# Key-value state copies by sample and bias heads by two, given out over eight projection rounds

## The chip, the cores and the metric

The kernel runs on one core of one Trainium2 chip. The metric is device time in microseconds, median of the runs. TensorE does the matrix products, VectorE and ScalarE move and convert tiles, GpSimd issues stores, SyncE issues loads. Loads and stores that SyncE issues go through the DMA queue called q1 in the profile, those that ScalarE issues through q10, those of GpSimd through q0. All three queues are served by the same 16 DMA engines.

## The reference

One inference step of a two-layer decoder trunk, for a prompt group of 512 rows and a sample group of 8 rows (520 columns in all). Layer 0 is attention with sparse branches; before it stands one large input projection. Layer 1 is a gated short convolution. What matters here:

```python
def att_project(h, w_in):
    proj = h @ w_in                 # 520 x 2048 by 2048 x P_ATT
...
def att_sample(h, ..., s_win_k, s_win_v, ...):
    k_w = jnp.concatenate([s_win_k, kw], axis=1)
    v_w = jnp.concatenate([s_win_v, vw], axis=1)
...
    return out, (kc, vc, ks, vs, k_w[:, tn:], v_w[:, tn:], kb, vb, ki)
...
def dense_attention(q, t, k, v, s, tbl, window):
    n = t[:, None] - s[None, :]
    bias = jnp.transpose(tbl[rel_bucket(n)], (0, 2, 3, 1))[None]
```

So two outputs, the window states of keys and of values, are the old states shifted by one row: for each of 8 samples, 511 rows of 256 numbers are copied unchanged from input to output, 4088 KB for each state. And the softmax logits get a bias that depends on the distance of query and key, one table for each of 16 heads.

## The kernel before

The program is a sequence of stages with a barrier of all engines between them. The change lies in `stage_project`, the second stage, which runs from about 130 to 1030 us of the span. It computes the input projection as 66 tiles of 128 output columns. For each tile, 2048 x 128 weights (1 MB) are loaded into one of four buffers `k.w`. ScalarE makes a high part of them (`Split.hi`, L128, writes `w_high`), VectorE the low part (`Split.lo`, L133, writes `w_low`), and TensorE multiplies in three passes (L146: 16 row blocks, 3 products, 2 halves of the columns). ScalarE copies one half of the result out of PSUM (L609), VectorE the other (L646), and GpSimd stores the tile to `k.proj` (L672).

Between the projection tiles the stage computes the modulation vectors of adaLN: one slot for each of tiles 0 to 63, with 1 MB of `w_ada` loaded into the same ring of four buffers and 16 small matmuls (L178). So a projection tile takes two entries of the ring, and the ring holds the entries of two tiles. Four tiles and four slots are one round. After the fourth tile of a round ScalarE also copies the round's modulation rows out (L185, `keep_rows`), and a round later TensorE turns them (L192).

All loads stand in one order on SyncE (L155): for each tile its projection weights, then its modulation weights. Each is issued when the buffer has come free, the projection weights' buffer by `w_low` and the modulation weights' buffer by the slot's last matmul.

The rounds run in segments, `SEGS`: a segment of one round is written out, one of more rounds is a loop on each engine. Before, these are rounds 0, 1 to 3, 4, 5 to 13, and 14 and 15. Between segments an engine may do something more.

In program order ScalarE does for tile t: `hi` of tile t + 1 (it waits for the load and for tile t - 1's matmuls), then the copy out of tile t. Whatever stands in ScalarE's order ahead of a `hi` delays the high part, then the low part, then TensorE.

Two blocks of DMAs stand in ScalarE's order, and nothing inside the stage reads what they write:

- `spread`, behind round 3 (tile 15). It stores the table of 16 bias heads (640 numbers each) to DRAM, waits for it to land, then issues 16 DMAs, one for each head, that write the head 128 times with a row step of 641 into `bias_skew` (320 KB each, DRAM to DRAM, L626). Stage `stage_attend_prompt` reads them a millisecond and more later.
- `move`, behind round 4 (tile 19). It issues two DMAs, DRAM to DRAM, each of 8 samples x 511 rows x 256 numbers (L618).

At the end of the stage ScalarE waits until all of them have landed.

Of the kernel before, what the change touches and what calls it, by code (L numbers as in the profile page):

```python
# [19 lines left out]
P = 128  # L20
D = 2048
# [3 lines left out]
NS = 8  # L25
# [4 lines left out]
NH = 8  # L30
# [4 lines left out]
WIN = 512  # L35
# [32 lines left out]
BREV = 640  # L68
# [300 lines left out]
def project_entry(t):  # L369

    return 32 + 8 * (t // 4) + 2 * (t % 4) if t < 64 else 160 + t - 64
# [147 lines left out]
def stage_project(k):  # L519
# [4 lines left out]
    gate_w_in, moved, hot_in, heads_mm, heads_kept, heads_out = (k.sem("pj_" + n) for n in ("gate_w_in", "moved", "hot_in", "heads_mm", "heads_kept", "heads_out"))  # L524
    sp_ = Split(k, project_entry, 2)

    SEGS = [(0, 1, 0, 0, 2 * D), (1, 4, 512, 0, 2 * D + 512), (4, 5, 2048, 1, 0), (5, 14, 2584, 1, 512), (14, 16, 7208, 1, 10 * 512)]

    def rounds(eng, body, *more):
        for seg in SEGS:  # L530
            if seg[1] - seg[0] == 1:
                body(0, seg)
            else:
                with eng.Fori(0, seg[1] - seg[0]) as j:
                    body(j, seg)
            for at, what in more:
                if at == seg[1]:
                    what()

    with ExitStack() as ctx:  # L540
# [5 lines left out]
        with nc.Block() as block:  # L546

            @block.sync
            def _(sp):
                w = k.i["w_in_att"]  # L550

                def body(j, seg):
                    first, _, col, layer, acol = seg
                    for s in range(4):
                        if first == 0 and s < 2:
                            continue
                        n = project_entry(4 * first + s)
                        load_weights(k, sp, n, w[0, :, bass.ds(j * 512 + (col + s * P), P)], j, 2)
                        load_weights(k, sp, n + 1, k.i["w_ada"][layer, s * 512:(s + 1) * 512, bass.ds(j * 512 + acol, 512)], j, 2)

                rounds(sp, body)
                load_weights(k, sp, project_entry(64), w[0, :, RUNS[2][1] + 8 * P:RUNS[2][1] + 9 * P])
                n = project_entry(65)
                sp.wait_ge(k.w_free[n % 4], n // 4)
                wg = k.w[:, n % 4, :].rearrange("p (a n) -> p a n", n=P)
                sp.dma_start(wg[:, :, 0:WI_ROW], k.i["w_in_att"][0, :, GA_COL:GA_COL + WI_ROW].rearrange("(a p) n -> p a n", p=P)).then_inc(k.w_in[n % 4], 16)
                sp.dma_start(wg[:, :, WI_ROW:P], k.i["w_in_att"][0, :, WI_COL:WI_COL + NI].rearrange("(a p) n -> p a n", p=P)).then_inc(gate_w_in, 16)
# [32 lines left out]
            @block.scalar  # L600
            def _(act):

                def step(t, j, first=False, last=False):
                    if not last:
                        sp_.hi(act, t + 1, j)
                    act.wait_ge(sp_.used, j * 4 + (t + 3))
                    if not first:
                        act.wait_ge(stored[t % 4], j * 16 + 16 * (t // 4))
                    nc.scalar.activation(out[:, t % 4, 0:HC], ps[:, t % 2 * 2, 0:HC], ACT.Copy).then_inc(kept_a, 1)  # L609

                def body(j, seg):
                    for s in range(4):
                        step(4 * seg[0] + s, j, first=(seg[0] == 0))
                    ada.keep_rows(act, project_entry(4 * seg[0] + 3) + 1, seg[0], j, 2)

                def move():
                    for name in ("win_k", "win_v"):
                        act.dma_start(k.o[name + "_s"][0, :, 0:WIN - 1], k.i["state_nsa_" + name][0, :, 1:WIN]).then_inc(moved, 16)  # L618

                def spread():  # L620

                    act.wait_ge(heads_kept, 2)
                    act.dma_start(k.bias_heads.rearrange("(h c) -> h c", c=BREV), heads[:, :]).then_inc(heads_out, 16)
                    act.wait_ge(heads_out, 16)
                    for h in range(2 * NH):
                        act.dma_start(bass.AP(k.bias_skew.tensor, h * P * (BREV + 1), [[BREV + 1, P], [1, BREV]]), bass.AP(k.bias_heads.tensor, h * BREV, [[0, P], [1, BREV]])).then_inc(moved, 16)  # L626

                act.dma_start(k.table[:, :], k.i["rel_bias"]).then_inc(hot_in, 16)
                act.dma_start(hot[:, :], k.i["hot"][:, 0:T]).then_inc(hot_in, 16)
                sp_.hi(act, 0)  # L630
                rounds(act, body, (4, spread), (5, move))
                act.wait_ge(gate_w_in, 16)
                step(64, 0)
                step(65, 0, last=True)
                act.wait_ge(moved, 32 + 16 * 2 * NH)

            @block.vector
            def _(dve):
# [1591 lines left out]
def build(nc, ins, outs):  # L2230
    with ExitStack() as ctx:
# [25 lines left out]
        with ExitStack() as layer0:  # L2257
# [4 lines left out]
            with ExitStack() as projecting:  # L2262
                k.split_buffers("0", projecting)
                with k.stage():
                    stage_front(k)
                with k.stage():
                    stage_project(k)
# [108 lines left out]
```

## Time and profile before

| | |
|---|---|
| median of 3 runs | 3528.1 us (3526.4 to 3530.64) |
| profiled execution, its own time | 3524.6 us |
| its span | 3523.0 us |
| granted TensorE clock, mean | 0.914 |
| TensorE matmul busy | 3045.3 us (86%) |
| DMA, mean over the span | 144 GB/s |

The profile gives, for one execution, each engine's instructions with start and duration, what ended the idle time before them, and the DMA packets by queue. The granted clock is that of TensorE: 1.00 is its upper level of 2.4 GHz and 0.50 its lower one of 1.2 GHz. A matmul's end is modelled, so a busy TensorE need not be one at its peak. DMA shares are of all 16 engines over the stretch. Packets are what one DMA engine moves in one piece.

### The profile page before, as it was taken

How to read it: one execution, taken by the hardware profiler on the slowest of the kernel's cores; microseconds unless marked ns; L12 is line 12 of the kernel's file. 1: busy time of each engine (PE TensorE's matmuls, PEld its weight loads, DVE VectorE, ACT ScalarE, POOL GpSimd, SP SyncE). 2: the span in 40 equal slices, each digit the busy share in tenths (PEclk: the TensorE clock that was granted, in tenths of full speed). 3: DMA queues.
4: the chain of work that ended last, by engine and by line, in shares of the span. 5: the costliest groups of instructions: out<-in, count | busy, mean ns of one | idle time of the engine just before them, and what ended most of it. 6: DMA issues, size and time to landing. Idle time of an engine off the chain costs nothing. (4 is left out here: it accounts for less than half of the span.)

```text
span 3523.0 us, 57162 instructions
## 1 busy us (share of the span) xinstructions
PE 3045.3 (86%) x22272; PEld 2671.5 (76%) x22272; DVE 1355.6 (38%) x2192; ACT 724.8 (21%) x1089; POOL 107.5 (3%) x149
## 2 busy tenths in 40 slices
PE   6799789999975889797886776699799999998796
PEld 3599779999963488685443554599799999998796
DVE  2321122212214278464342666622543344343333
ACT  2211111111102021220000433311422222221212
POOL 0000000000000000000000112100000000000000
PEclk8799889999987899998877886799999999999898
DMA  9766766666634641424977224431333333330621
GB/s 339 225 177 199 236 199 181 176 183 188 188 109 133 196 119 48 123 76 148 299 231 227 73 73 138 130 99 45 89 101 90 101 95 96 101 93 27 176 64 49
DMA packets 592962, 496.73 MB, mean 141 GB/s; under 512 B 36908, under 2 KB 515645, under 8 KB 591597
## 3 DMA queue, kind: packets, MB, share of 16 engines
q1 hardware_dynamic: 526872, 408.45, 39.8%
q10 hardware_dynamic: 58128, 60.58, 5.3%
q0 software_dynamic: 7840, 26.10, 1.8%
q8 instruction: 73, 1.20, 0.1%
q14 instruction: 49, 0.40, 0.0%
HBM read 460.02 MB, written 48.70 MB: 144 GB/s over the span
## 5 line engine op out<-in xcount | busy, mean ns | idle before, releaser
L146 PE MATMUL psum<-h_high,w_high 128*128 128x260 f32 x5184 | 1057.9, 285 | 106.6 <-DVE w_low L133 56.2
L146 PE MATMUL psum<-h_high,w_low 128*128 128x260 f32 x5184 | 1049.2, 284 | 0.0
L146 PE MATMUL psum<-h_low,w_high 128*128 128x260 f32 x5184 | 1047.8, 284 | 0.0
L146 PEld LDWEIGHTS psum<-h_high,w_high 128*128 128x128 f32 x5184 | 804.5, 190 | 150.4 <-issue 93.7
L146 PEld LDWEIGHTS psum<-h_high,w_low 128*128 128x128 f32 x5184 | 804.2, 190 | 0.0
L146 PEld LDWEIGHTS psum<-h_low,w_high 128*128 128x128 f32 x5184 | 803.3, 190 | 0.0
L133 DVE TENSOR_TENSOR w_low<-w,w_high 128x2048 fp32r<-128x2048 f32 x162 | 371.0, 2291 | 580.0 <-ACT w_high L128 579.7
L128 ACT ACTIVATE w_high<-w 128x2048 fp32r<-128x2048 f32 x162 | 309.3, 1910 | 500.5 <-PE psum L146 391.6
L646 DVE COPY pj_out<-psum 128x260 f32<-128x260 f32 x66 | 28.3, 429 | 525.8 <-PE psum L146 525.8
L609 ACT ACTIVATE pj_out<-psum 128x260 f32<-128x260 f32 x66 | 25.6, 387 | 673.0 <-PE psum L146 673.0
L178 PE MATMUL psum<-w,c 128*32 128x512 f32 x768 | 110.7, 659 | 29.6 <-DMA w<-in_w_ada 21.0
L1395 DVE COPY at_kt<-psum 128x512 f32<-128x512 f32 x144 | 93.4, 686 | 63.1 <-PE psum L1466 62.6
L1078 PE MATMUL psum<-w,cz_xtk 128*128 128x256 f32 x512 | 117.2, 390 | 0.0
L1078 PE MATMUL psum<-w_v,cz_xtv 128*128 128x256 f32 x512 | 117.2, 390 | 0.0
L1078 PEld LDWEIGHTS psum<-w,cz_xtk 128*128 128x128 f32 x512 | 115.3, 308 | 0.4
L1078 PEld LDWEIGHTS psum<-w_v,cz_xtv 128*128 128x128 f32 x512 | 115.3, 308 | 0.4
L1994 DVE TENSOR_TENSOR ou_t<-psum,adaT 128x8 f32<-128x8 f32 x32 | 5.3, 166 | 232.5 <-PE psum L146 232.5
L2160 DVE RECIPROCAL cv_parts<-cv_parts 128x520 f32<-128x520 f32 x16 | 54.4, 3402 | 78.9 <-ACT cv_parts L2114 78.9
L1731 PE MATMUL psum<-pa_ptA,pa_vA 128*128 128x128 f32 x320 | 54.6, 308 | 16.5 <-ACT pa_ptA L1773 16.5
L1731 PEld LDWEIGHTS psum<-pa_ptA,pa_vA 128*128 128x128 f32 x320 | 46.7, 215 | 26.4 <-ACT pa_ptA L1773 21.5
L672 POOL DMA_DIRECT2D proj<-pj_out x66 | 35.9, 544 | 987.9 <-DVE pj_out L646 987.9
L868 PE MATMUL psum<-ip_k,ip_q 128*128 128x128 f32 (+3 forms) x128 | 38.5, 455 | 30.1 <-DMA ip_q<-proj 30.1
(361 smaller groups left out, 2667.1 us busy)
## 6 DMA issues: line engine op xcount, KB each, us to landing
w<-in_w_ada SPq DMA_DIRECT2D x96, 1024.0 KB, 6.3
w<-in_w_in_att SPq DMA_DIRECT2D x65, 1024.0 KB, 9.2
w<-in_w_in_conv SPq DMA_DIRECT2D x64, 1024.0 KB, 6.3
proj<-pj_out POOLq DMA_DIRECT2D x66, 260.0 KB, 5.4
cz_pgk<-in_cache_nsa_cmp_k SPq DMA_DIRECT2D x128, 128.0 KB, 2.2
cz_pgv<-in_cache_nsa_cmp_v SPq DMA_DIRECT2D x128, 128.0 KB, 2.2
w<-in_w_out_att SPq DMA_DIRECT2D x16, 1024.0 KB, 6.0
w<-in_w_out_conv SPq DMA_DIRECT2D x16, 1024.0 KB, 6.1
```

The costliest lines, as they stand in the source:

```text
L128: act.activation(k.wh[:, s % 2, :], k.w[:, n % 4, :], ACT.Copy).then_inc(self.high, 1)
L133: dve.tensor_tensor(k.wl[:, s % 2, :], k.w[:, n % 4, :], k.wh[:, s % 2, :].bitcast(F32), ALU.subtract).then_inc(k.w_free[n % 4], 1)
L146: mm = pe.matmul(k.psum[:, banks + hf, 0:HC], w[:, kt, :], x[:, kt, hf * HC:(hf + 1) * HC], start=(kt == 0 and m == 0), stop=(kt == KT - 1 ...
L178: mm = pe.matmul(k.psum[32 * a:32 * a + 32, self.bank, :], k.c32[:, q * 4 + a, :], k.w[:, n % 4, a * 512:(a + 1) * 512], start=(q == 0), s ...
L609: nc.scalar.activation(out[:, t % 4, 0:HC], ps[:, t % 2 * 2, 0:HC], ACT.Copy).then_inc(kept_a, 1)
L646: dve.tensor_copy(out[:, t % 4, HC:TC], ps[:, t % 2 * 2 + 1, 0:HC]).then_inc(kept_v, 1)
L672: pool.dma_start(tile, out[:, t % 4, :]).then_inc(stored[t % 4], 16)
L868: mm = pe.matmul(ps[:, 4 * b + i, 0:P * (i + 1)], q[:, b, i * P:(i + 1) * P], ki[:, 0:P * (i + 1)], start=True, stop=True)
L1078: mm = pe.matmul(ps[:, b, 0:CH], rows, w1[:, l, :], start=(l == 0), stop=(l == CB - 1))
L1395: eng.tensor_copy(kt[:, s % 2, :, c * 256:(c + 1) * 256], ps[:, 3 + q % 2, :].rearrange("p (g q) -> p g q", g=G)).then_inc(kept, 1)
L1731: mm = pe.matmul(ps[:, o, i * P:(i + 1) * P], hv[:, r % SL, br, c, :], pt[:, v % ring, c * P:(c + 1) * P], start=(not A and v % UH == 0 an ...
L2160: dve.reciprocal(e[:, :], e[:, :]).then_inc(zrecip, 1)
```

## The change

The DMAs of both blocks are given out over rounds 5 to 12. At the end of each of these rounds, behind `keep_rows`, ScalarE issues four DMAs: the key state and the value state of one sample (sample j in the j-th of these rounds), and two bias heads (2j and 2j + 1). The store of the head table stays behind round 3, without the wait for its landing; this wait now stands in each round ahead of the bias heads' DMAs. To get a segment of eight rounds, round 13 becomes a segment of its own. The bytes that are moved, and all that is computed, are the same. The bias heads' access patterns are written in another form with the same rows of 640 numbers.

```diff
-    SEGS = [(0, 1, 0, 0, 2 * D), (1, 4, 512, 0, 2 * D + 512), (4, 5, 2048, 1, 0), (5, 14, 2584, 1, 512), (14, 16, 7208, 1, 10 * 512)]
+    SEGS = [(0, 1, 0, 0, 2 * D), (1, 4, 512, 0, 2 * D + 512), (4, 5, 2048, 1, 0), (5, 13, 2584, 1, 512), (13, 14, 2584 + 8 * 512, 1, 9 * 512), (14, 16, 7208, 1, 10 * 512)]
...
                     ada.keep_rows(act, project_entry(4 * seg[0] + 3) + 1, seg[0], j, 2)
-
-                def move():
-                    for name in ("win_k", "win_v"):
-                        act.dma_start(k.o[name + "_s"][0, :, 0:WIN - 1], k.i["state_nsa_" + name][0, :, 1:WIN]).then_inc(moved, 16)
-
-                def spread():
-
+                    if seg[0] == 5:
+                        copies(j)
+
+                def pass_heads():
                     act.wait_ge(heads_kept, 2)
                     act.dma_start(k.bias_heads.rearrange("(h c) -> h c", c=BREV), heads[:, :]).then_inc(heads_out, 16)
+
+                def copies(j):
+
+
+                    for name in ("win_k", "win_v"):
+                        act.dma_start(k.o[name + "_s"][0, bass.ds(j, 1), 0:WIN - 1], k.i["state_nsa_" + name][0, bass.ds(j, 1), 1:WIN]).then_inc(moved, 16)
                     act.wait_ge(heads_out, 16)
-                    for h in range(2 * NH):
-                        act.dma_start(bass.AP(k.bias_skew.tensor, h * P * (BREV + 1), [[BREV + 1, P], [1, BREV]]), bass.AP(k.bias_heads.tensor, h * BREV, [[0, P], [1, BREV]])).then_inc(moved, 16)
+                    skew = k.bias_skew.rearrange("(h p c) -> h p c", p=P, c=BREV + 1)
+                    rows = k.bias_heads.rearrange("(h c) -> h c", c=BREV).unsqueeze(1)
+                    for i in range(2):
+                        act.dma_start(skew[bass.ds(j * 2 + i, 1), :, 0:BREV], rows[bass.ds(j * 2 + i, 1)].broadcast_to([1, P, BREV])).then_inc(moved, 16)
...
-                rounds(act, body, (4, spread), (5, move))
+                rounds(act, body, (4, pass_heads))
...
-                act.wait_ge(moved, 32 + 16 * 2 * NH)
+                act.wait_ge(moved, 16 * 4 * NS)
```

## Rows read from the trace of the kernel before

**Rows 1.** Stretches of the stage: us, busy us of each engine, granted clock, DMA share, GB/s
```profile
338.40:390.14 51.74, 44.04 (x350) 40.24 (x350) 9.99 (x9) 9.46 (x9) 2.17 (x4) 0.93 0.84 243
...
425.00:449.00 24.00, 3.41 (x16) 1.94 (x16) 0.00 (x0) 0.00 (x0) 0.00 (x0) 0.56 0.57 225
...
454.00:460.00 6.00, 6.00 (x34) 6.00 (x35) 2.59 (x3) 1.91 (x1) 0.54 (x1) 0.64 1.06 344
...
480.45:532.19 51.74, 51.74 (x428) 47.84 (x431) 10.99 (x9) 9.41 (x9) 2.17 (x4) 1.00 0.63 183
```

**Rows 2.** ScalarE in order of time, an undisturbed round: start us, us, instruction
```profile
480.45 0.39 ACT L609 ACTIVATE pj_out<-psum 128x260 f32<-128x260 f32 x1 [10.52 <-PE psum L146]
...
532.19 0.39 ACT L609 ACTIVATE pj_out<-psum 128x260 f32<-128x260 f32 x1 [10.52 <-PE psum L146]
533.30 0.60 ACT L185 ACTIVATE ada_rows<-psum 128x512 f32<-128x512 f32 x1 [0.72 <-PE psum L178]
533.79 1.92 ACT L128 ACTIVATE w_high<-w 128x2048 fp32r<-128x2048 f32 x1
```

**Rows 3.** ScalarE in order of time, the last undisturbed round's end
```profile
997.85 0.39 ACT L609 ACTIVATE pj_out<-psum 128x260 f32<-128x260 f32 x1 [10.52 <-PE psum L146]
```

**Rows 4.** ScalarE in order of time, round 4, behind the bias heads' DMAs
```profile
338.40 0.39 ACT L609 ACTIVATE pj_out<-psum 128x260 f32<-128x260 f32 x1 [10.52 <-PE psum L146]
...
344.13 11.14 ACTq L626 DMA_DIRECT2D bias_skew<-bias_heads  x16
355.38 1.91 ACT L128 ACTIVATE w_high<-w 128x2048 fp32r<-128x2048 f32 x1 [15.28 <-issue]
...
399.24 0.39 ACT L609 ACTIVATE pj_out<-psum 128x260 f32<-128x260 f32 x1 [10.52 <-PE psum L146]
```

**Rows 5.** ScalarE in order of time, round 5, behind the states' DMAs
```profile
400.27 0.79 ACTq L618 DMA_DIRECT2D out_win_k_s<-in_state_nsa_win_k  x1
401.10 0.71 ACTq L618 DMA_DIRECT2D out_win_v_s<-in_state_nsa_win_v  x1
402.08 1.92 ACT L128 ACTIVATE w_high<-w 128x2048 fp32r<-128x2048 f32 x1 [1.21 <-issue]
412.03 0.39 ACT L609 ACTIVATE pj_out<-psum 128x260 f32<-128x260 f32 x1 [8.04 <-PE psum L146]
449.64 1.91 ACT L128 ACTIVATE w_high<-w 128x2048 fp32r<-128x2048 f32 x1 [37.23 <-DMA w<-in_w_in_att]
```

**Rows 6.** Waits of TensorE, first in 340 to 380 us, then in 400 to 480: total, times, longest
```profile
PE psum L146 <- DVE w_low L133: 7.7, 1, 7.7
...
PE psum L146 <- DVE w_low L133: 23.3, 1, 23.3
PE psum L178 <- DMA w<-in_w_ada: 2.6, 1, 2.6
```

**Rows 7.** SyncE's issues in order of time: start us, us that the issue took
```profile
339.42 0.37 SPq L155 DMA_DIRECT2D w<-in_w_ada  x1
339.83 0.51 SPq L155 DMA_DIRECT2D w<-in_w_in_att  x1
...
413.10 31.35 SPq L155 DMA_DIRECT2D w<-in_w_ada  x1
```

**Rows 8.** DMA queues, 400 to 450 us: packet sizes, then queue, packets, MB, share
```profile
DMA packets 3431, 11.91 MB, mean 238 GB/s; under 512 B 88, under 2 KB 2257, under 8 KB 3302
...
q10 hardware_dynamic: 144, 8.37, 38.7%
```

**Rows 9.** DMA queues, 340 to 400 us
```profile
q10 hardware_dynamic: 2336, 5.28, 30.3%
```

**Rows 10.** DMA in 505.87 to 557.61 us, an undisturbed round: tenths in 40 slices, landing
```profile
DMA  0469999800008899993000599999100269999900
...
w<-in_w_in_att SPq DMA_DIRECT2D x4, 1024.0 KB, 9.1
```

**Rows 11.** The bias heads' DMAs by tile name: issue ns min/median/max
```profile
L626 ACTq DMA_DIRECT2D bias_skew<-bias_heads x16: 612/619/1388, 344.1 to 353.9; - x16
```

## The prediction

> **What bounds the kernel now.** I read the busy time by stretches over the projection stage first, then ScalarE's instructions in order of time, then TensorE's waits, then the DMA queues. In an undisturbed round TensorE is busy for 51.74 of 51.74 us at the full granted clock, and the 16 DMA engines are busy for 0.63 of it [rows 1]. So the stage is bound by TensorE's matmuls. The copies out of PSUM by ScalarE are a clock for it: they mark the end of each tile. The ends of round 5 and round 6 are 532.19 - 480.45 = 51.74 us apart [rows 2], and the nine rounds up to 997.85 us take (997.85 - 532.19) / 9 = 51.74 us each [rows 3]. Nothing is to be won or lost there except by keeping TensorE waiting.
>
> Two rounds are not like that. Round 4 ends 399.24 - 338.40 = 60.84 us after round 3 [rows 4], which is **9.1 us** over the normal 51.74. Round 5 ends 480.45 - 399.24 = 81.21 us after round 4 [rows 2, 4], **29.5 us** over. Together 38.6 us of an otherwise even stage. They have different causes, and it matters which part of the change removes which.
>
> *Round 4 is late because of ScalarE's order, not of bandwidth.* A `hi` normally starts 533.79 - 532.19 = 1.60 us after the last copy of a round [rows 2], so here it should start at 340.00. It starts at 355.38, behind the wait for the head table and 11.14 us of issuing 16 DMAs [rows 4]: 15.4 us late. TensorE then waits 7.7 us for `w_low` [rows 6]. So a `hi` at this place may come 15.4 - 7.7 = **7.7 us** late before TensorE notices. The other 1.4 us of the 9.1 is the granted clock, 0.93 in this round [rows 1].
>
> *Round 5 is late because of the transfers.* Issuing the two state copies took 0.79 + 0.71 us, the `hi` behind them came at 402.08, and the next copy out came 412.03 - 399.24 = 12.79 us after the last [rows 4, 5], a normal tile. The damage comes after it: SyncE's next load issue is held for 31.35 us [rows 7], a `hi` waits 37.2 us for its weights [rows 5], TensorE waits 23.3 + 2.6 us [rows 6], and its granted clock is 0.56 from 425 to 449 us and still 0.64 from 454 to 460 [rows 1]. That the clock falls to its lower level of 1.2 GHz while TensorE idles is part of the 29.5 us, since I read the loss from tile ends.
>
> What the copies do to the DMA engines: q10 moves 8.37 MB in 144 packets and takes 38.7% of 16 engines in 50 us, which is 0.387 x 50 x 16 = **310 engine-us** [rows 8]. 3431 - 3302 = 129 packets of all queues are 8 KB and longer, so the data went in about 128 packets of 65 KB, 2.4 us each. The stall of 37 us fits these 310 engine-us spread over 8 engines (38.7 us), one for each sample, and not over 16 (19.4 us). For most of this time the loads behind them hardly move. The bias heads took 0.303 x 60 x 16 = **291 engine-us** on q10 [rows 9], in packets of 5.28 MB / 2336 = 2.3 KB.
>
> **The change, part by part.**
>
> *Removed behind round 3.* The wait for the head table and the 16 issues go; one issue of the head table stays. The `hi` there returns to its place and 9.1 us are gained, with the clock's dip.
>
> *Removed behind round 4.* Both state copies go, with the 29.5 us and the clock that they cost.
>
> *Added: ScalarE's issue time in rounds 5 to 12.* Behind `keep_rows`, ahead of the next `hi`: two state issues of at most 0.79 and 0.71 us [rows 5] and two bias heads at 0.619 us median [rows 11], 2.7 us together. The upper bound takes the longest seen for all four, 4 x 1.39 = 5.6 us [rows 11]; the issues now compute their addresses from the loop counter, which no ScalarE row here shows (SyncE's, which do the same, take 0.37 us [rows 7]). Both ends are under the 7.7 us of slack. What is queued behind them is one `hi`, then VectorE's `lo`, then TensorE's next tile but one; the running tile is their cover. Cost nothing; the price beyond 7.7 us would be 8 times the excess. The wait for the head table in each round is for a store issued over 100 us before: nothing.
>
> *Added: DMA work in rounds 5 to 12.* Each round gets an eighth of both: 310 / 8 = 38.7 and 291 / 8 = 36.4 engine-us, 75 in all. A round has 51.74 x 16 = 828 engine-us and uses 0.63 of them, 522; with the copies 597, or 0.72. There is room on the average. But it could be late in one burst, so the slack of one load counts. The load of projection weights issued at 339.83 [rows 7] lands 9.1 us later by the median [rows 10], at 348.9. It is used by the `hi` behind the copy out of the next tile, which is due 12.79 us after the copy at 338.40, at 351.2, and 0.3 us later begins: 2.6 us of slack, and then the 7.7 us that a `hi` has. A load may be **10.3 us** late. If all of a round's copies stood ahead of it on evenly used engines, it would be 75 / 16 = 4.7 us late. If the state copies fell on 8 engines, as they do now, it would be 38.7 / 8 + 36.4 / 16 = 7.1 us. Both are covered; the digits of the round show two to four empty slices of 1.3 us behind each tile's loads [rows 10], and there the engines catch up before the next tile. I take nothing, with an upper end of 2.5 us a round, 20 us, for a share that lies badly. Less than nothing isn't possible, as undisturbed rounds have TensorE busy throughout.
>
> *How many engines one sample's copy takes* is the one number that the trace doesn't show, since here each copy has 8 samples. The Trainium skill, "DMA: Bandwidth & Descriptors", section "Why a DMA increments its semaphore by 16 and not by 1", says that a DMA is spread over the largest k up to 16 that divides the slowest dimension larger than 1, and that a contiguous run in a single dimension can be cut so that it spreads. By that rule the copy before has k = 8, for its 8 samples, and the trace agrees (310 engine-us in a stall of about 37 us). For one sample it would give 16 if the run is cut, and if it is not, 1; the sum above would stand with 16 and fall with 1, and no row here shows which.
>
> *The segments.* Round 13 written out in place of a pass of the loop costs nothing: the stretch from 532.19 to 997.85 us crosses such a border, behind round 13, at an even 51.74 us a round [rows 2, 3].
>
> *The end of the stage.* The last copies are issued behind round 12, three rounds (155 us) ahead of the wait for them. Nothing.
>
> *The sum* against the profiled execution: 3524.6 - 9.1 - 29.5 = 3486.0 us. The runs' median is 3.5 us above that execution, so the forecast for the median is 3528.1 - 38.6 = 3489.5; with half a microsecond for small delays, **3490.0**.
>
> **The rivals.**
>
> *A. The copies leak.* Both stalls go, but in each of the eight rounds TensorE waits a little: a load comes more than 10.3 us late, or a `hi` more than 7.7. For: loads and copies will be issued side by side, since SyncE's loads come 1.4 us behind a round's last copy out (339.83 against 338.40) and ScalarE's DMAs 1.0 us behind it (400.27 against 399.24) [rows 4, 5, 7]; the round's DMA share rises to 0.72, and a held SyncE issue delays all later ones in its order [rows 7]. Against: the sums above leave 3 us even at 8 engines. At 0.5 to 2.5 us a round it gives 3494 to 3510.
>
> *B. One sample's copy runs on one engine.* The place: the engine that gets all of it. It has 0.63 x 51.74 = 32.6 us of weights and stores in a round, plus 38.7 us of states, plus 2.3 us of bias heads: 73.6 us, against 51.74. Each weight load is spread over all engines and complete only when the slowest has done its part, so each round would last 73.6 us at least: 8 x 21.9 = 175 us more, 3490 + 175 = 3665 us. If weights stand still while such a copy runs, as they do now, each round costs what `move` costs now, 29.5 us, and the time is 3490 + 236 = 3726. The point from which it decides is the load's slack: 38.7 / n + 2.3 exceeds 10.3 us for n of 4 engines and fewer; at 4 it is 1.7 us a round, a case of A, at 2 it is 11.4 us a round, 91 us. Against: 8 packets of 65 KB for each sample could as well go to 8 engines, and an even cut is natural for a contiguous run. The skill's rule named above gives this result if the run isn't cut. Time 3665 to 3726, slower.
>
> *C. Issuing costs more inside the loop.* If the four issues take more than 7.7 us, the stall of round 4 comes back eight times. At 9 us, 1.3 x 8 = 10 us plus clock dips of 1.4 x 8 = 11: 3511. Against: 1.39 us is the longest of 16.
>
> *D. It doesn't do what it says.* The stalls would have to come from something that stays. Both begin right behind the moved instructions, and the undisturbed rounds before and after have none; if only the 9.1 us went, the time would be 3519.
>
> **How the numbers follow.** Forecast, 3484 to 3494: 0.70. A: 0.14. B, with two engines as well, which ends slower too: 0.08. C: 0.05. D: 0.03. Predicted time 3490.0. The range 3484 to 3511 holds the forecast, most of A and part of C, about 0.85. A measurement of this kernel can tell 0.2%, 7 us, from no change; B alone ends slower, and of A, C and D only a few hundredths lie near zero: faster 0.90, within 0.2% 0.02, slower 0.08.
>
> **What would show it.** Right: all rounds 51.7 us apart; no wait of TensorE for `w_low` over 1 us in the stage; granted clock 1.00 from 184 us to the stage's end; DMA share near 0.72 in rounds 6 to 13; about 3 us of issuing behind each `keep_rows` and a `hi` about 5 us behind the round's last copy out; no SyncE issue over a few us. Wrong: rounds 6 to 13 evenly longer, with a `hi` waiting for `w` (A or B; the length and number of q10's packets tell them apart) or with the `hi` late by issue (C). It would also be wrong if a later stage changed its length, for which I have no reason.

## The result

The changed kernel takes **3484.0 us** (median of 4 runs, 3478.7 to 3486.9) against 3527.7 us before (3526.4 to 3530.6 in the 4 runs of this comparison): ratio 0.9873, 95% interval 0.9856 to 0.9890. That is 43.8 us less. The forecast was 3490.0 (a gain of 38.6 us, less half a microsecond for small delays), with a range that began at 3484. The median lies 6.0 us under the forecast and a hair outside the range (unrounded 3483.99), and the gain is 5 us larger than the sum says. The profiled execution took 3484.61 us, 40.0 under that of before.

Stretches of the projection stage, after (us, busy us of PE, PEld, DVE, ACT, POOL, granted clock, DMA share, GB/s); rounds 4, 5, 6 and 7. They answer to [rows 1]:

```profile
338.90:390.64 51.74, 51.74 (x428) 47.84 (x431) 11.08 (x10) 9.47 (x10) 2.17 (x4) 1.00 0.64 185
390.64:442.38 51.74, 51.74 (x428) 47.85 (x431) 10.99 (x10) 9.35 (x10) 2.16 (x4) 1.00 0.64 184
442.38:494.12 51.74, 51.74 (x428) 47.85 (x431) 10.99 (x10) 9.59 (x10) 2.16 (x4) 1.00 0.71 216
494.12:545.86 51.74, 51.74 (x428) 47.84 (x431) 10.99 (x10) 9.58 (x10) 2.16 (x4) 1.00 0.72 216
```

Rounds 4 and 5, 60.84 and 81.21 us before, are 51.74 us like their neighbours, the clock stays at its upper level, and the DMA share in the rounds with copies is 0.71 to 0.72. TensorE waits for nothing between 150 and 960 us. ScalarE in order of time, after, at the end of round 6; it answers to [rows 2, 4, 5]:

```profile
494.12 0.39 ACT L609 ACTIVATE pj_out<-psum 128x260 f32<-128x260 f32 x1 [10.52 <-PE psum L146]
495.22 0.60 ACT L185 ACTIVATE ada_rows<-psum 128x512 f32<-128x512 f32 x1 [0.72 <-PE psum L178]
495.45 0.54 ACTq L626 DMA_DIRECT2D out_win_k_s<-in_state_nsa_win_k  x1
496.24 0.54 ACTq L626 DMA_DIRECT2D out_win_v_s<-in_state_nsa_win_v  x1
497.02 1.36 ACTq L631 DMA_DIRECT2D bias_skew<-bias_heads  x2
498.91 1.92 ACT L128 ACTIVATE w_high<-w 128x2048 fp32r<-128x2048 f32 x1 [3.09 <-issue]
506.91 0.39 ACT L609 ACTIVATE pj_out<-psum 128x260 f32<-128x260 f32 x1 [6.08 <-PE psum L146]
511.91 1.92 ACT L128 ACTIVATE w_high<-w 128x2048 fp32r<-128x2048 f32 x1 [4.61 <-DMA w<-in_w_in_att]
519.53 0.39 ACT L609 ACTIVATE pj_out<-psum 128x260 f32<-128x260 f32 x1 [5.70 <-PE psum L146]
```

The four issues and what lies between them take 2.9 us (495.45 to 498.38), and the `hi` behind them starts 4.8 us behind the round's last copy out where 1.6 is normal. The next `hi` waits 4.6 us for its weights, which are late because of the copies. Both delays are used up before TensorE: the copies out are 12.79 and 12.62 us apart. DMA queues in this round, after (kind: packets, MB, share of 16 engines):

```profile
q10 hardware_dynamic: 352, 1.70, 8.8%
```

0.088 x 51.74 x 16 = 73 engine-us, where the forecast had 75. The 1.05 MB of the two states went in 32 packets of 32.7 KB, which is each state cut into 16. They took 38.8 engine-us between 500.31 and 503.39 us, so at least 13 engines ran at once: the copy of one sample runs on 16 engines, not on 8 and not on one.

So the projection stage did what the forecast said, within 0.2 us. From barrier to barrier it takes 869.5 us instead of 908.3, 38.8 less. What is left open is the other part of the gain, and it lies outside the stage. The stage of mixer A's prompt attention, whose program text is the same, took 204.9 us before and 201.9 after.

### The profile page after: what moved, and what is told of

It is laid out like the page before. It is cut to its first block and busy times, and to the rows that moved or that the text cites. A ratio compares the mean times of both kernels' runs of the same rounds, so it can differ in the third digit from the quotient of the medians.

```text
span 3483.0 us, 57217 instructions
## 1 busy us (share of the span) xinstructions
PE 3043.6 (87%) x22272; PEld 2668.6 (77%) x22272; DVE 1355.1 (39%) x2192; ACT 726.5 (21%) x1089; POOL 107.2 (3%) x149
## 5 line engine op out<-in xcount | busy, mean ns | idle before, releaser
L873 PE MATMUL psum<-ip_k,ip_q 128*128 128x128 f32 (+3 forms) x128 | 39.0, 459 | 29.9 <-DMA ip_q<-proj 29.9
```

The costliest lines, as they stand in the source:

```text
L873: mm = pe.matmul(ps[:, 4 * b + i, 0:P * (i + 1)], q[:, b, i * P:(i + 1) * P], ki[:, 0:P * (i + 1)], start=True, stop=True)
```

## The experiments

Each run was timed beside the kernel before on the same chip; "before" below is its median there. The length of a stage is read from barrier to barrier in the profiled execution.

### Is the surplus real, and do the two halves add up?

The changed kernel once more:

> The changed kernel once more, timed in five rounds beside the kernel before. The forecast's sum (theory S: the two stalls of 9.1 and 29.5 us and nothing else) gives before minus 38.6 us. The first comparison gave 3527.7 - 3484.0 = 43.8 us, 5 us more. If this surplus is only the spread of a few executions (theory N), the difference here lies between 37 and 41 us. If something in later stages is really faster (theory L), it is again 42 to 46 us, and the prompt attention stages are again 3.0 and 1.7 us shorter in the trace than before.

Measured: 3482.0 us against 3524.4, 42.4 less, ratio 0.9883 (0.9868 to 0.9899). Projection stage 869.5 us; mixer A's prompt attention 201.3. The surplus is there again, as theory L said. The interval of this one comparison, 35.6 to 46.5 us, holds 38.6 too, so by itself it doesn't rule out chance; the comparisons below do.

The halves alone. Only the states given out:

```diff
                     act.dma_start(k.bias_heads.rearrange("(h c) -> h c", c=BREV), heads[:, :]).then_inc(heads_out, 16)
+                    act.wait_ge(heads_out, 16)
+                    for h in range(2 * NH):
+                        act.dma_start(bass.AP(k.bias_skew.tensor, h * P * (BREV + 1), [[BREV + 1, P], [1, BREV]]), bass.AP(k.bias_heads.tensor, h * BREV, [[0, P], [1, BREV]])).then_inc(moved, 16)
 
                 def copies(j):
...
-                    act.wait_ge(heads_out, 16)
...
-                    for i in range(2):
-                        act.dma_start(skew[bass.ds(j * 2 + i, 1), :, 0:BREV], rows[bass.ds(j * 2 + i, 1)].broadcast_to([1, P, BREV])).then_inc(moved, 16)
```

> Only the state copies are given out over the rounds; the 16 bias heads stay in one block behind round 3. By the forecast only the stall of round 5 goes: 29.5 us less than before, and round 4 keeps its 9.1 us (ScalarE's hi 15 us late, TensorE waiting 7.7 us for w_low). If the two stalls had one common cause in the DMA queues, round 4's stall would shrink or the gain would not be 29.5 us.

Measured: 3492.9 us, 31.6 less than before's 3524.4, ratio 0.9901 (0.9886 to 0.9916). Stage 880.9 us, 27.4 less than 908.3; round 5 is 51.74 us long, round 4 is 62.93 (340.42 to 403.35), a stall of 11.2 us and not of 9.1.

And only the bias heads given out (`move` as before, behind round 4):

> Only the bias heads are given out, two a round; the state copies stay in one block of two DMAs behind round 4. By the forecast 9.1 us less than before, round 4 at 51.74 us and round 5 still about 81 us long. The sum of this gain and that of the other half is 38.6 us if the parts are independent.

Measured: 3509.9 us, 14.5 less, ratio 0.9962 (0.9949 to 0.9976). Stage 900.6 us, 7.7 less; round 4 is normal, round 5 takes 81.5 us, a stall of 29.8. The two stalls are separate, as the forecast had them. But the halves gain 31.6 and 14.5 us by their times and 27.4 and 7.7 by their stages, and both stage gains lie under the intervals of the times (29.6 to 40.2 and 8.5 to 18.0 us). The surplus stands in both halves, which speaks against either group of DMAs as its cause.

Does it hang on when the later stages start?

```diff
...
                 act.wait_ge(moved, 16 * 4 * NS)
+                act.wait_ge(sp_.used, NTILES + 2)
+                for i_ in range(20):
+                    act.wait_ge(idled, (i_ + 1))
+                    act.activation(idle[:, :].rearrange("p (a n) -> p a n", n=T), k.xT[:, 0:4, 0:T], ACT.Copy).then_inc(idled, 1)
```

> The changed kernel with 20 activations of 1.9 to 2.0 us each, one after another, on ScalarE at the end of the projection stage, all other engines idle: 38 to 40 us are put back, so that the later stages start about when they do in the kernel before. Theory S or N: the time is that of the changed kernel plus the 38 to 40 us, so 0 to 2 us from before. Theory L with a cause in what the change left behind for later stages: about 5 us under before still. Theory L with a cause in when the later stages start (the granted clock in the attention stages, where it moves between its two levels): the surplus goes and the time is before's.

Measured: the 20 activations take 38.8 us, but 7.6 us of that lie beside the last tile's store; the stage takes 900.7 us, 31.2 more than in the changed kernel. Time 3514.4 us, 10.1 under before, where its stage is 7.6 under 908.3. Against the changed kernel it is 32.3 us longer for 31.2 us of stage. The later stages now start within 8 us of where they do before and their surplus is 2.5 us by this count, which is too little to tell by time. The trace tells more: mixer A's prompt attention takes 200.2 us, as in the changed kernel, so the start time isn't what makes it shorter.

### Where the surplus comes from

All variants so far share one thing beside the DMAs, the new segments. Two kernels test it: the kernel before again, and the kernel before with this line alone:

```diff
-    SEGS = [..., (5, 14, 2584, 1, 512), (14, 16, 7208, 1, 10 * 512)]
+    SEGS = [..., (5, 13, 2584, 1, 512), (13, 14, 2584 + 8 * 512, 1, 9 * 512), (14, 16, 7208, 1, 10 * 512)]
```

> The kernel before, profiled a second time. The stage of mixer A's prompt attention took 204.9 us in the first trace of before and 199.6 to 201.9 in the five traces of the changed kernel and its variants so far. Theory N (the granted clock of that stage differs from run to run, whatever the kernel): it lies between 199 and 205 us here, as like to be low as high. Theory P (something in the program of before makes it longer): about 205 us again.

> The kernel before with the new segments alone: round 13 written out, no DMA moved. All variants so far have these segments, and all their later stages together were about 4 us shorter than before's by the medians. The forecast prices the segments at nothing: the projection stage as long as before, 908 us, and the time within 2 us of before's. Theory P with the program's layout as its cause (code lies at other addresses in all later stages): 3 to 5 us less than before, outside the projection stage.

Measured: before again 3524.8 us, ratio 0.9997 (0.9988 to 1.0007), that attention stage 203.4 us. Segments alone **3517.3 us, 7.8 less, ratio 0.9974 (0.9965 to 0.9982)**, the stage 197.7 us. No DMA is moved, and still it is faster. (The projection stage of this execution is not shorter but 3.4 us longer than 908.3, in the two stalls.) The step "The segments" of the forecast is the one that fails.

The trace shows the place. VectorE in that stage, the kernel before (start us, us, instruction, idle time before it and what ended it):

```profile
2030.07 0.29 DVE L1790 CUSTOM_DVE_ANT_0 pa_sA<-psum,pa_tA 128x128 f32<-128x128 f32 x1 [3.08 <-issue]
...
2034.18 0.11 DVE L1827 MEMSET pa_lcA<- 128x64 f32 x1 [3.62 <-issue]
```

and TensorE behind it:

```profile
2037.17 1.02 PE L1711 MATMUL psum<-const,pa_lcA 128*16 128x128 f32 x4 [5.53 <-DVE pa_lcA L1851]
```

The same three places with the segments alone:

```profile
2030.71 0.29 DVE L1790 CUSTOM_DVE_ANT_0 pa_sA<-psum,pa_tA 128x128 f32<-128x128 f32 x1 [2.55 <-issue]
...
2031.31 0.11 DVE L1827 MEMSET pa_lcA<- 128x64 f32 x1
```

```profile
2034.31 1.02 PE L1711 MATMUL psum<-const,pa_lcA 128*16 128x128 f32 x4 [2.54 <-DVE pa_lcA L1851]
```

"issue" means that the engine waited for nothing that the profile shows. Before, VectorE stands 3.08 us and then again 3.62; with the segments, once, 2.55. TensorE's wait for the result shrinks by 3.0 us. It isn't a hidden wait for TensorE: the one product that the program makes the memset wait for (`cqk`, L1699) was ready at 2026.49 us, over 7 us before the memset. The waits of VectorE for "issue" in this stage (total us, times, longest) are, in the kernel before:

```profile
DVE pa_lcA L1827 <- issue: 4.1, 2, 3.6
DVE pa_sA L1790 <- issue: 3.1, 1, 3.1
```

and in the changed kernel:

```profile
DVE pa_sA L1795 <- issue: 2.5, 1, 2.5
```

7.2 us against 2.5: **4.7 us**. It is the same in three traces of before, and like the changed kernel (2.5 to 2.8 us, no wait ahead of the memset) in all 13 traces of kernels with the new segments in VectorE's program. The whole stage agrees: with VectorE's old program it takes 203.1 to 206.0 us in five traces, with the new one 197.4 to 202.1 in 13, and the means are 4.6 us apart.

What moves it? Every engine has its own program, so round 13 can be written out for one engine and left in the loop for another (`for seg in (SPLIT if eng is nc.vector else ONE_LOOP)` and its opposite). Three kernels, the third being the changed kernel with VectorE's loop left as it was:

> The kernel before, with round 13 written out in VectorE's program alone; the other engines keep the loop of nine rounds, no DMA is moved. In both traces of before VectorE stands 4.1 to 4.2 us (twice) ahead of its memset of pa_lcA in the prompt attention stage, waiting for nothing that the profile shows, and in none of eight traces of kernels with the new segments. Theory V (where VectorE's instructions lie in its own program decides this): the standstill is gone, that stage takes 198 to 202 us and not 203 to 205, and the kernel is 4 to 8 us faster than before. Theory W (it hangs on another engine's program or on the whole program's length): the standstill stays and the time is before's.

> The kernel before, with round 13 written out in every engine's program but VectorE's. Theory V: the standstill of 4.1 us stays and the time is within 2 us of before's. Theory W: it goes, and the kernel is 4 to 8 us faster. If TensorE's 197 added instructions had a share of their own, the time would lie between.

> The changed kernel, but VectorE keeps its loop of nine rounds as before; all DMAs are given out as in the changed kernel. Theory V: the standstill of 4.1 us is back, and the gain over before is the forecast's 38.6 us (37 to 40.5), not 42 to 44. Theory W: as the changed kernel, 3482 us or 42 to 44 us under before.

Measured, with before at 3527.9 us:

| round 13 written out | time | ratio, 95% interval | that stage |
|---|---|---|---|
| for VectorE alone | 3520.2 us | 0.9980 (0.9971 to 0.9989) | 199.4 us |
| for all but VectorE | 3526.1 us | 0.9994 (0.9985 to 1.0003) | 204.8 us |
| changed kernel, all but VectorE | 3485.1 us | 0.9882 (0.9867 to 0.9897) | 203.1 us |

The waits for "issue", in this order:

```profile
DVE pa_sA L1791 <- issue: 2.5, 1, 2.5
```

```profile
DVE pa_lcA L1828 <- issue: 4.6, 2, 4.1
DVE pa_sA L1791 <- issue: 3.1, 1, 3.1
```

```profile
DVE pa_lcA L1833 <- issue: 4.1, 2, 3.6
DVE pa_sA L1796 <- issue: 3.1, 1, 3.1
```

The standstill follows VectorE's program and nothing else, each time as theory V said. The written-out round has 15 rows of VectorE's in the trace (9 of them work on tiles) and 424 matmuls with as many weight loads of TensorE's: the few take the standstill away, the many don't. (The 197 of the expectation stands in no trace.) The third kernel's time is a miss: 42.8 us under before, where 37 to 40.5 were expected. Timed beside it, the changed kernel with the same packets (`states_on_4_engines` below) took 3481.3 us, 3.8 less than its 3485.1, which is the right sign and near 4.7 us; but both are medians of four runs, and the interval of its gain, 36.3 to 46.9 us, holds 38.6 as well as 43.3. So that the standstill costs time is shown on the kernel before, where VectorE's program alone is worth 7.7 us; how much of the changed kernel's surplus it makes up is not.

Why it stands: in the traces an 8 KB packet of the DMA queue named "instruction" runs inside each such standstill. Queues in the kernel before from 2026.9 to 2030.1 us, and from 2030.5 to 2034.1:

```profile
q14 instruction: 2, 0.02, 2.1%
```

```profile
q14 instruction: 1, 0.01, 1.1%
```

With the segments alone there is one in the remaining gap (2028.1 to 2030.7 us) and the second gap is not there. That VectorE waited for its own next instructions, and that a few more of them moved a border of such a block away from this place, fits all of it. But a packet of this queue doesn't always go with a standstill: with the segments alone one runs at 2033.06 us, while VectorE works on without a gap, and the profile doesn't say for which engine a packet is. That the standstill follows VectorE's layout is shown; that the packet is the cause is only argued from its timing.

A third trace of before, to see how much its two stalls spread:

> The kernel before, profiled a third time. Rounds 4 and 5 together lost 38.6 us in both traces of before, and 38.2, 41.7 and 41.8 us in three kernels that issue the same blocks of DMAs. If that is spread from one execution to the next, this trace may show either 38 or 42 us, and the mean of them, about 40, is what the forecast should have put down; if the program decides it, it is 38.6 again. VectorE's standstill ahead of its memset of pa_lcA is 4.1 us again by theory V.

Measured: 3527.8 us, ratio 1.0006 (0.9996 to 1.0016). Rounds 4 and 5 lost 38.5 us (their `keep_rows` start 141.95 us apart, against 2 x 51.74), and the standstill is 4.1 us. So the three traces of before agree on 38.5 to 38.6. In two of the three kernels that issue the same blocks and differ only in the segments it was 41.7 and 41.8 us (38.2 in the third), the excess being in round 4. Over all seven traces that keep the block of bias heads, round 4 takes 60.3 to 60.8 us where the engines other than VectorE keep the loop of nine rounds (before three times, and `split_vector_only`), and 62.9 to 63.5 where they don't (`segments_only`, `split_all_but_vector`, `states_in_rounds`). The block itself is slower there: the `hi` behind it starts 17.8 to 18.7 us after the last copy out and not 15.9 to 17.0, TensorE waits 8.5 to 9.4 us for `w_low` and not 6.6 to 7.7, and the granted clock of the round is 0.92 and not 0.94. So this too seems to go with a program's layout, perhaps ScalarE's; no run tests it, and it can't touch the changed kernel, which has no such block.

### Are the prices of the stalls right?

The forecast had a slack of 7.7 us for a `hi` behind a round, 10.3 us for a load, and a rule: the loads stand still for as long as the copies ahead of them take on their engines. First the `hi`, made later by activations behind each round's DMAs (two and four of them):

> The changed kernel with two more activations (1.94 us each, one after another) on ScalarE behind each round's four DMAs, so the next hi comes 3.2 + 3.9 = 7.1 us later than in an undisturbed round. By the forecast's slack of 7.7 us TensorE doesn't notice: rounds of 51.7 us, the time of the changed kernel. If the slack is smaller by more than a microsecond, each of eight rounds is longer by the excess.

> The same with four activations: the hi comes 3.2 + 7.8 = 11.0 us late, 3.3 over the slack of 7.7. By the forecast's rule eight rounds lose 3.3 us each, 26 us, and up to 1.4 us more each for the granted clock, 26 to 38 us in all. If ScalarE's order had no such edge (VectorE or TensorE could run on), less.

Measured: with two 3482.7 us (0.9882, 0.9863 to 0.9900), stage 869.5 us, the `hi` 6.5 us late and no wait of TensorE. With four 3504.0 us (0.9931, 0.9916 to 0.9946), about 22 over the changed kernel. Its rows:

```profile
499.10 0.39 ACT L610 ACTIVATE pj_out<-psum 128x260 f32<-128x260 f32 x1 [10.52 <-PE psum L146]
...
503.46 7.76 ACT L620 ACTIVATE pj_idle<-xT 128x2048 f32<-128x2048 f32 x4 [2.65 <-issue]
511.12 1.89 ACT L128 ACTIVATE w_high<-w 128x2048 fp32r<-128x2048 f32 x1
```

The `hi` comes 12.02 - 1.60 = 10.4 us late, so 10.4 - 7.7 = 2.7 us should show. TensorE's waits in the stage:

```profile
PE psum L146 <- DVE w_low L133: 22.6, 8, 3.5
```

Seven of the eight waits are 2.7 to 2.8 us, and there the clock stays at 1.00 and the round is 2.8 us longer. In the first round the `hi` was 11.2 us late; TensorE waited 3.5 us, the granted clock of that round was 0.97, and the round was 4.9 us longer. So the slack of 7.7 us is right to a tenth at both latenesses, and the further 1.4 us for the clock came with the wait of 3.5 us and not with those of 2.8. The stage is 24.7 us longer than in the changed kernel, a little under the 26 to 38 expected.

Then the load. The first try wrote each sample's state as 4 rows:

> The changed kernel, with each sample's state written as 4 rows of two pieces of 65 KB, so that the copy runs on 4 DMA engines. The forecast's rule for a load's slack: the loads behind the copies are late by 38.7 / 4 + 2.3 = 12.0 us where 10.3 are covered, so TensorE waits 1.7 us in each of eight rounds, 14 us, and up to 1.4 us more each for the granted clock: 3496 to 3507 us. If loads stood still for less than the copies' whole time, the time is that of the changed kernel, 3482; if a held issue of SyncE costs more than the copy's own time, it is more than 3510.

Measured: 3481.3 us, ratio 0.9867 (0.9852 to 0.9882), but it tests nothing: the trace has 32 packets of 32.7 KB a round on 16 engines, as in the changed kernel. Here a contiguous run was cut in the same way when it was written down as 4 rows. It counts as one more run of the changed kernel. So the next two copy rows that aren't contiguous, 63 rows of 4 (or 2) samples at a time:

```diff
                     for name in ("win_k", "win_v"):
-                        act.dma_start(k.o[name + "_s"][0, bass.ds(j, 1), 0:WIN - 1], k.i["state_nsa_" + name][0, bass.ds(j, 1), 1:WIN]).then_inc(moved, 16)
+                        for b in range(0, NS, 4):
+                            act.dma_start(k.o[name + "_s"][0, b:b + 4, bass.ds(j * 63, 63)], k.i["state_nsa_" + name][0, b:b + 4, bass.ds(j * 63 + 1, 63)]).then_inc(moved, 16)
```

> The changed kernel, but each round copies 63 rows of 4 samples at a time (two DMAs for each state; 7 rows remain and go out behind round 13). The slowest dimension is 4, so each DMA runs on 4 engines, the same ones, with packets of 64.5 KB. By the forecast's rule the loads are late by 38.7 / 4 + 2.3 = 12.0 us, 1.7 over the slack, 14 to 25 us over eight rounds: 3496 to 3507 us. The issues cost 4 x 0.55 + 1.4 = 3.6 us, covered. If the rule is too strict (the loads behind go on while the copies run): 3482.

> The same with 2 samples at a time, four DMAs for each state, on 2 engines. The loads are late by 38.7 / 2 + 2.3 = 21.7 us, 11.4 over the slack: 91 us over eight rounds, 102 with the clock, 3573 to 3584 us. ScalarE's issues take 8 x 0.55 + 1.4 = 5.8 us, still under 7.7. If loads on the other engines went on and only two engines' shares were late by turns, the load on these two engines decides: 32.6 + 19.4 + 2.3 = 54.3 us in a round of 51.74, 2.5 us a round, 20 us, 3502.

Measured: on 4 engines 3477.5 us, ratio 0.9865 (0.9848 to 0.9881), stage 870.1 us, TensorE waits for nothing. On 2 engines **3571.1 us, ratio 1.0126 (1.0107 to 1.0145)**, stage 959.2 us, 89.7 more than the changed kernel. SyncE's issues around the copies, on 2 engines (start us, us that the issue took):

```profile
520.76 13.34 SPq L155 DMA_DIRECT2D w<-in_w_ada  x1
534.29 2.06 SPq L155 DMA_DIRECT2D w<-in_w_in_att  x1
536.53 5.03 SPq L155 DMA_DIRECT2D w<-in_w_ada  x1
```

and TensorE's waits in its eight rounds:

```profile
PE psum L146 <- DVE w_low L133: 72.1, 16, 8.7
```

In both kernels a round has 16 packets of 64.5 KB. They take 10.6 us from first to last on 4 engines and 20.9 on 2, near to 38.3 / 4 = 9.6 and 39.1 / 2 = 19.5 us for their engine-us, so the copies do run on so many engines.

The loads go the way that the forecast named: a held issue of SyncE stops them on all engines, as [rows 7] showed for 31.35 us. While it is held, hardly a byte of q1 moves. The queues in the kernel before from 415 to 440 us, and on 2 engines from 522 to 533 us:

```profile
q10 hardware_dynamic: 88, 5.23, 48.4%
q1 hardware_dynamic: 88, 0.10, 1.1%
```

```profile
q10 hardware_dynamic: 16, 0.52, 10.9%
q1 hardware_dynamic: 16, 0.01, 0.2%
```

So the other half of the engines, or the other 14, stand nearly idle. A load of projection weights that SyncE issued beside such copies took 30.4 us to land (median 9.1 in [rows 10]), 21.3 late for 21.7 by the rule:

```profile
w<-in_w_in_att SPq DMA_DIRECT2D x1, 1024.0 KB, 30.4
```

The milder account (two engines' own load, 20 us) is refuted. The stage's 89.7 us are close to the 91 us that the forecast gave to rival B at that point, but in part by luck: those 91 us were waiting alone, and TensorE waited 72.1 us; the rest goes with the clock, 0.92 from 500 to 900 us. In each round the first wait, 0.5 to 1.0 us, belongs to ScalarE, whose ten issues make the `hi` 8.3 us late; the second, 8.2 to 8.7 us, is the load's. Together they are 72.1 / 8 = 9.0 us for loads 21.7 us late, so the slack of a load is about 12.7 us, and the 12.0 us at 4 engines pass under it; the forecast had 10.3. It took the 7.7 us of the first `hi` of a round for that of the next one. The next one started 19.1 us late where TensorE was 9.0 us late, a slack of 10.0.

Last, is it the giving out or the engines? All 16 state copies of one sample each, but in one block behind round 4:

> The changed kernel, but all 16 state copies (8 samples, two states, one DMA each) are issued in one block behind round 4, as before; the bias heads stay given out. Each copy now runs on 16 engines. The forecast's account of the 29.5 us stall (310 engine-us on 8 engines, 38.7 us) says that on 16 engines they take 19.4 us, of which a load's slack covers 10.3: 9 us of stall. ScalarE issues for 8.8 us, 1 to 2 over its slack, within the same time. With the clock's dip 9 to 12 us over the changed kernel: 3492 to 3496. If giving out over rounds were what matters and not the engines, about 29.5 us: 3512.

Measured: 3492.6 us, ratio 0.9907 (0.9892 to 0.9922). The round takes 66.95 us (`keep_rows` at 392.71 and 459.66), a stall of 15.2 us against 29.5 to 29.9 with 8 engines; TensorE waits 11.4 us of it (2.8 for the `hi` behind the 16 issues, 8.7 for a load), the rest goes with the clock, 0.85 from 395 to 440 us. The time is in the expected 3492 to 3496 us, the stage's stall above the 9 to 12: the copies took 27.0 us from first to last where 19.4 were summed, since a packet of 32.7 KB took 1.46 us on average and not 1.21 as in the changed kernel. So about half of `move`'s stall goes when the copies run on 16 engines instead of 8. The rest goes only when they are given out, and 2.8 us of it are the price of issuing 16 DMAs in place of two.

## Why the forecast was right and wrong

*Bound and stalls: right.* TensorE's matmuls bound the stage, two rounds were late by 9.1 and 29.5 us for two different causes, and both went. The stage gained 38.8 us for 38.6 forecast, and the halves alone gave 7.7 and 27.4 us of stage.

*Issue time: right.* 2.9 us behind each round where 2.7 were summed, and the slack of 7.7 us that covers it holds (no wait with two activations more, 2.7 to 2.8 us a round with four, as far as the `hi` was 10.4 us late).

*DMA work: right in sum, its edge too strict.* 73 engine-us a round for 75, share 0.72 for 0.72. The term that was mis-sized is the slack of a load: about 12.7 us and not 10.3. It didn't move the forecast, since both cover the 4.7 us.

*How many engines: right choice, 16.* The Trainium skill's rule ("DMA: Bandwidth & Descriptors", section "Why a DMA increments its semaphore by 16 and not by 1"), that a contiguous run in a single dimension can be cut so that it spreads, holds here for one sample's run: 16 packets of 32.7 KB for each state, at least 13 engines at once. Rival B was no idle fear: on 2 engines it costs 89.7 us of stage.

*The segments: wrong, and this is the step that failed.* "Round 13 written out in place of a pass of the loop costs nothing" was argued from the projection stage alone, and of later stages the forecast said that it had no reason to expect a change. The line moves all that follows in each engine's program. One standstill of VectorE in a later stage, 4.7 us, goes with it. Alone it is worth 7.8 us by its time (6.3 to 12.3), written out for VectorE alone 7.7 us (3.9 to 10.2). The sum with this term, 38.6 + 4.7 = 43.3 us, gives 3484.8 us; measured were gains of 43.8, 42.4 and 46.6 us in the three comparisons of the same DMAs. The changed kernel with the standstill put back gained 42.8, so that this term alone closes the gap isn't shown. The lower end of the range, too, rested on the belief that nothing could be gained beyond the stalls ("Less than nothing isn't possible"); it left 6 us below the forecast, where four runs of one kernel spread over 8 (3478.7 to 3486.9).

What stays open: the segments' gain by time (7.8 and 7.7 us) is 3 us larger than the 4.7 us of the trace, the changed kernel without this gain is still 42.8 us faster and not 38.6, and three traces had 2 to 3 us more of stall in round 4. The intervals of these times are 6 to 11 us wide and leave room for chance in the first two.

## What to carry to other kernels

A copy that nobody waits for can still stop the loads behind it, for as long as its slowest engine needs; once that exceeds the slack of one load, the bound engine waits. So look at how many engines it takes, then give it out in shares under that slack. In front of an in-order engine's critical instruction, measure the slack once from an existing stall (lateness minus the wait of the bound engine): it held to a tenth, but for that instruction only, as the next one had 2.3 us more. And where a change lengthens an engine's program, count the waits for "issue" in all later stages before and after, since they can come and go with the layout.

## What the hardware showed that was not expected

- VectorE stood still for 3.6 to 4.1 us in mid-stage, with an 8 KB packet of the instruction queue inside the gap, in all five traces with one layout of its program and in none of the 13 with the other; one written-out round of 15 rows, some 1100 us earlier, decided.
- A copy in 65 KB packets on 8 engines kept the other queue's loads off all 16 for nearly the whole of its time (q1 1.1% against q10 48.4% from 415 to 440 us), and copies of 64.5 KB packets on 2 engines did it too (0.2% against 10.9%): SyncE's next issue itself took 31.35 and 13.3 us, against 0.37 us normally.
- TensorE's granted clock stayed at its upper level through seven waits of 2.7 to 2.8 us (1.00 over 400 us), was 0.97 in a round with one of 3.5 us, and fell to 0.56 in the stretch with the wait of 23.3 us [rows 1, 6]. With the copies in a block on 16 engines it was 0.81 from 405 to 414 us, around a wait of 2.8 us, so the length of a wait alone doesn't decide.
